# The head of the first feed-forward part in quarter pieces over two issuing queues, and the rounded half of a weight unit waited for alone

## What is computed

```
def swiglu(x, w_gate, w_up, w_down):
    return (jax.nn.silu(x @ w_gate) * (x @ w_up)) @ w_down
h = h + FFN_RES * swiglu(rms_norm(h, ffn1_norm[l]), ...)
h = h + hybrid_mixer(rms_norm(h, mix_norm[l]), ...)
h = h + FFN_RES * swiglu(rms_norm(h, ffn2_norm[l]), ...)
```

## Time and profile before

| | us |
|---|---|
| median of three runs | 1114.24 |
| profiled execution, its own time | 1114.35 |
| its span | 1112.5 |
| around the span | 1.85 |
| PE busy | 1106.8 (99%) |
| DVE busy | 790.6 (71%) |
| ACT busy | 621.2 (56%) |
| transfers, mean over the span | 187 GB/s |

### The profile page before, as it was taken

How to read it: one execution, slowest core, us unless ns; L and a number is a source line. 1 busy time by engine, 2 the same in 40 slices (tenths; PEclk the granted TensorE clock), 3 DMA queues, 4 the chain that set the end, 5 groups by cost and what they waited for, 6 DMA issues and landing times.

```text
span 1112.5 us, 14865 instructions
## 1 busy us (share of the span) xinstructions
PE 1106.8 (99%) x5830; PEld 941.2 (85%) x5830; DVE 790.6 (71%) x1136; ACT 621.2 (56%) x825; POOL 58.0 (5%) x105
## 2 busy tenths in 40 slices
PE   9999999999999999999999999999999999999998
PEld 8888888888888888888888888888877788888887
DVE  6777754667987677775477787557898786777752
ACT  6556542677656456554356556337787854656530
POOL 1000000100000000000000000011343000000000
PEclk9999999999999999999999999999999999999999
DMA  9755565654454665555565555557643455555541
GB/s 317 252 190 189 189 246 190 211 162 141 165 195 157 203 189 190 189 189 189 191 206 190 189 189 189 189 154 255 224 150 122 149 181 164 191 188 194 192 179 38
DMA packets 142581, 208.02 MB, mean 187 GB/s; under 512 B 9296, under 2 KB 100584, under 8 KB 142512
## 3 DMA queue, kind: packets, MB, share of 16 engines
q1 hardware_dynamic: 139408, 198.07, 52.7%
q0 software_dynamic: 3088, 9.00, 2.4%
q10 hardware_dynamic: 16, 0.00, 0.0%
HBM read 205.98 MB, written 2.65 MB: 188 GB/s over the span
## 4 chain that ended last, share of the span: by engine, by line
PE 98%; ACT 1%; DMA 0%; issue 0%; DVE 0%; SPq 0%; ACTq 0%; DVEq 0%
PE banks L1810 28%; PE banks L1696 16%; PE banks L1698 16%; PE banks L1697 16%; PE banks L1807 14%; PE banks L1768 1%; PE banks L2046 1%; PE banks L1718 1%; PE banks L1983 1%; DMA raw<-in_ffn_w_gate 0%; PE banks L2076 0%; PE banks L2073 0%; PE banks L2142 0%; PE banks L2016 0%; PE banks L2019 0%
## 5 line engine op out<-in xcount | busy, mean ns | idle before, releaser
L1143 DVE TENSOR_TENSOR w_lo<-raw,w_hi 128x2048 fp32r<-128x2048 f32 x186 | 422.7, 2275 | 167.8 <-ACT w_hi L752 167.5
L752 ACT ACTIVATE w_hi<-raw 128x2048 fp32r<-128x2048 f32 x186 | 352.2, 1897 | 111.8 <-PE banks L1698 108.2
L1810 PE MATMUL banks<-xT,w_hi 128*128 128x512 f32 x1344 | 314.5, 390 | 0.0
L1810 PEld LDWEIGHTS banks<-xT,w_hi 128*128 128x128 f32 x1344 | 249.2, 188 | 49.7
L1696 PE MATMUL banks<-w_hi,xT 128*128 128x512 f32 (+1 forms) x432 | 170.4, 394 | 0.0
L1807 PEld LDWEIGHTS banks<-xT,w_lo 128*128 128x128 f32 x1344 | 167.4, 191 | 3.4
L1807 PE MATMUL banks<-xT,w_lo 128*128 128x256 f32 x1344 | 169.8, 283 | 0.0
L1698 PE MATMUL banks<-w_hi,xT 128*128 128x512 f32 (+1 forms) x432 | 167.0, 387 | 0.0
L1697 PE MATMUL banks<-w_lo,xT 128*128 128x512 f32 (+1 forms) x432 | 166.7, 386 | 0.0
L1696 PE MATMUL banks<-w_hi,hT_hi 128*128 128x512 f32 x352 | 137.3, 390 | 0.0
L830 ACT ACTIVATE gate<-gate 128x256 f32<-128x256 f32 x84 | 35.1, 418 | 182.5 <-DVE gate L1272 182.5
(11 more groups left out here) (324 smaller groups left out, 900.1 us busy)
## 6 DMA issues: line engine op xcount, KB each, us to landing
raw<-in_ffn_w_gate SPq DMA_DIRECT2D x88, 512.0 KB, 3.7
raw<-in_ffn_w_up SPq DMA_DIRECT2D x88, 512.0 KB, 4.7
raw<-in_ffn_w_down SPq DMA_DIRECT2D x88, 512.0 KB, 4.1
raw<-in_w_in SPq DMA_DIRECT2D x76, 512.0 KB, 4.4
raw<-in_w_out SPq DMA_DIRECT2D x16, 512.0 KB, 4.0
raw<-in_w_branch_moba SPq DMA_DIRECT2D x4, 512.0 KB, 4.4
raw<-in_w_branch_sb SPq DMA_DIRECT2D x4, 512.0 KB, 4.9
raw<-in_w_branch_a SPq DMA_DIRECT2D x4, 512.0 KB, 4.2
```

The costliest lines, as they stand in the source:

```text
L752: act.activation(w_hi[u % SLOTS][:, 0:n], raw[u % RAWS][:, 0:n], ACT.Copy).then_inc(hi_done, 1)
L1143: dve.tensor_tensor(w_lo[r][:, 0:n], raw[r][:, 0:n], w_hi[u % SLOTS][:, 0:n], ALU.subtract).then_inc(lo_done, 1)
L1810: m = pe.matmul(bank[b + s], mh, xT[:, k].rearrange("p a s -> p (a s)"), start=first, stop=k == KC - 1, skip_group_check=c == 0)
```

## The change

1. x comes in four transfers of 256 columns instead of two of 512. The gate and up halves of unit 0 and 1 come in two pieces each (`load_first`, 256 KB), but unit 1's up pieces share one semaphore.
2. SP issues x's first quarter ahead of the identity. The gate half of unit 0 is issued by ACT, one piece ahead of the gain rows and one behind them.
3. PE transposes two column groups, starts on unit 0's gate after them, and takes the rest a quarter at a time. The second column group has a bank of its own (`first_bank`) and is rounded by DVE (`second_hi`).
4. ACT and DVE round and subtract the gate half of both units and the up half of unit 0 in pieces.
5. `pair_chunk` waits for `hi_done` of its first unit, and for `lo_done` only ahead of the products of `w_lo`, in 40 chunks.
6. GpSimd waits for `hi_done` of unit 3 ahead of the positions and tables too.

The core of the diff (semaphores, DVE's half and the removed functions left out):

```
...
+        def load_first(eng, u, s, i, signal):
+
+            w = a[ffn_w[0][s]].rearrange("(k p) (c n) -> p k c n", p=P, n=CH)
+            k = 4 * u + 2 * i
+            eng.dma_start((gate_half, up_half)[s](raw[u])[:, 2 * i:2 * i + 2, :], w[:, k:k + 2, 0, :]).then_inc(signal, 16)
+
+        def first_bank(k):
+
+            return bank[3][:, 0:SEQ] if k == 1 else bank[4 + k // 2][:, k % 2 * SEQ:(k % 2 + 1) * SEQ]
+
...
+            load_x(0)
             sp.dma_start(ident, a["consts"][:, 0:P]).then_inc(ident_in, 16)
-            load_x(0)
+            load_x(1)
+            for i in range(2):
+                load_first(sp, 0, 1, i, up_in[i])
+            for j in range(2, 4):
+                load_x(j)
+            for i in range(2):
+                load_first(sp, 1, 0, i, gate_in[1][i])
+            for i in range(2):
+                load_first(sp, 1, 1, i, raw_in[1])
...
             pool.memset(freq[:, 0:1], INV_FREQ[0]).then_inc(gained, 4)
+            pool.wait_ge(hi_done, 4)
...
+                    first_x_hi(0)
+                    act.wait_ge(first_half_hi[0], 1)
+                    gate_hi(0, 1)
+                    first_x_hi(1)
+                    for i in range(2):
+                        act.wait_ge(up_in[i], 16)
+                        act.activation(up_half(w_hi[0])[:, 2 * i:2 * i + 2, :], up_half(raw[0])[:, 2 * i:2 * i + 2, :],
+                                       ACT.Copy).then_inc(hi_done if i else up_hi, 1)
+                    for i in range(2):
+                        first_x_hi(2 + i)
+                        gate_hi(1, i)
+                    act.wait_ge(raw_in[1], landed(1))
+                    act.activation(up_half(w_hi[1]), up_half(raw[1]), ACT.Copy).then_inc(hi_done, 1)
...
             act.preload_act_table_set("silu_and_others")
+            load_first(act, 0, 0, 0, gate_in[0][0])
             act.dma_start(gain_rows, a[gains[0]].rearrange("(k p) -> k p", p=P)).then_inc(gain_row_in, 16)
+            load_first(act, 0, 0, 1, gate_in[0][1])
...
+                    dve.wait_ge(gate_in[0][0], 16)
+                    dve.tensor_copy(gate_half(w_hi[0])[:, 0:2, :], gate_half(raw[0])[:, 0:2, :]).then_inc(first_half_hi[0], 1)
+                    dve.wait_ge(second_turned, 1)
+                    dve.tensor_scalar(xT_hi[:, 1, :], first_bank(1), gain_cols[:, 1:2], None, ALU.mult).then_inc(second_hi, 1)
+                    for i in range(2):
+                        gate_lo(0, i)
+                        if i == 0:
+                            dve.wait_ge(second_hi, 1)
+                        first_x_lo(i)
...
+            def first_turn(j):
+
+                pe.wait_ge(x_in[j], 16)
+                for k in (2 * j, 2 * j + 1):
+                    for tt in range(TT):
+                        ins = pe.transpose(first_bank(k)[:, tt * P:(tt + 1) * P], x[:, tt, k * P:(k + 1) * P], ident)
+                    if k == 0:
+                        ins.then_inc(x_turned, 1)
+                    elif k == 1:
+                        ins.then_inc(second_turned, 1)
+                if j:
                     ins.then_inc(x_turned, 1)
+            def first_term(u, s, i, term):
+
+                j = 2 * u + i
+                if term == 0:
+                    pe.wait_ge(xT_hi_done, j + 1)
+                    if s == 0:
+                        pe.wait_ge(first_half_hi[u], i + 1)
+                    elif u == 0 and i == 0:
+                        pe.wait_ge(up_hi, 1)
+                    else:
+                        pe.wait_ge(hi_done, u + 1)
+                elif term == 1:
+                    if s == 0:
+                        pe.wait_ge(first_half_lo, j + 1)
+                    elif u == 0 and i == 0:
+                        pe.wait_ge(up_lo, 1)
+                    else:
+                        pe.wait_ge(lo_done, u + 1)
+                else:
+                    pe.wait_ge(xT_lo_done, j + 1)
+                last = u == 1 and s == 1 and term == 2 and i == 1
+                for k in (2 * j, 2 * j + 1):
+                    if k == 1 and s == 0 and term == 0:
+                        pe.wait_ge(second_hi, 1)
...
-                    first_columns(0, 0)
+                    first_term(0, 0, 0, 0)
                     first_turn(1)
-                    first_columns(0, 1)
-                    first_columns(1, 0)
-                    first_columns(1, 1)
+                    first_term(0, 0, 0, 1)
+                    first_term(0, 0, 0, 2)
+                    for term in range(3):
+                        first_term(0, 0, 1, term)
+                    first_term(0, 1, 0, 0)
+                    first_term(0, 1, 1, 0)
+                    first_turn(2)
+                    first_turn(3)
+                    first_term(0, 1, 0, 1)
+                    first_term(0, 1, 1, 1)
+                    first_term(0, 1, 0, 2)
+                    first_term(0, 1, 1, 2).then_inc(unit_used, 1)
+                    for s in range(2):
+                        for term in range(3):
+                            for i in range(2):
+                                m = first_term(1, s, i, term)
+                    m.then_inc(unit_used, 1)
...
                 u = BASE[ph] + 2 * c
-                pe.wait_ge(lo_done, u + 1)
+                pe.wait_ge(hi_done, u + 1)
                 for p in range(2):
                     pair_free(ph, c, p)
                     pair_products(ph, c, 0, p, False)
                 if c == 1 and ph not in FIRST_OF:
                     spread_rows(ph)
+                pe.wait_ge(lo_done, u + 1)
                 for p in range(2):
                     m = pair_products(ph, c, 0, p, True)
                 m.then_inc(unit_used, 1)
```

More of the change, by code:

```diff
@@ L327, in build @@
         tile_done = sem("tile_done")
-        first_half = [sem("first_half0"), sem("first_half1")]
+        gate_in = [[sem(f"gate_in{u}{i}") for i in range(2)] for u in range(2)]
+        up_in = [sem("up_in0"), sem("up_in1")]
+        up_hi = sem("up_hi")
+        second_turned = sem("second_turned")
+        second_hi = sem("second_hi")
+        up_lo = sem("up_lo")
         gain_row_in = sem("gain_row_in")
@@ L334, in build @@
         warm_set = sem("warm_set")
-        x_in = [sem("x_in0"), sem("x_in1")]
+        x_in = [sem(f"x_in{j}") for j in range(4)]
         ident_in = sem("ident_in")
@@ L579, in load_gate_up @@
                     w = a[ffn_w[f][s]].rearrange("(k p) (c n) -> p k c n", p=P, n=CH)
-                    put(u, slot[:, :, s * CH:(s + 1) * CH], w[:, 4 * hf:4 * hf + 4, c, :],
-                        first_half[u] if u < 2 and s == 0 else None)
+                    put(u, slot[:, :, s * CH:(s + 1) * CH], w[:, 4 * hf:4 * hf + 4, c, :])
             def load_rows(w, u, r0, rows, c0, width):
@@ L605, in _ @@
                     f = FFN_OF[ph]
-                    for c in range(1):
-                        for hf in range(2):
-                            load_gate_up(f, c, hf, u0 + 2 * c + hf)
-                            if ph == "F0" and hf == 0:
-                                load_x(1)
-                    for c in range(1, NCH):
+                    for c in range(ph == "F0", NCH):
                         for hf in range(2):
@@ L647, in zero_rest @@
                 ins.then_inc(zeroed, 1)
-            for n in range(2):
-                pool.wait_ge(x_in[n], 16)
+            for j in range(4):
+                pool.wait_ge(x_in[j], 16)
             pool.memset(freq[:, 0:1], INV_FREQ[0]).then_inc(gained, 4)
+            pool.wait_ge(hi_done, 4)
             for t in range(TT):
@@ L765, in first_x_hi @@
                 act.wait_ge(x_turned, j + 1)
-                for i in range(2):
-                    k = 2 * j + i
-                    ins = act.activation(xT_hi[:, k, :], bank[4 + j][:, i * SEQ:(i + 1) * SEQ], ACT.Copy,
-                                         scale=gain_cols[:, k:k + 1])
+                for k in (0,) if j == 0 else (2 * j, 2 * j + 1):
+                    ins = act.activation(xT_hi[:, k, :], first_bank(k), ACT.Copy, scale=gain_cols[:, k:k + 1])
                 ins.then_inc(xT_hi_done, 1)
@@ L840, in ffn, with gate_hi @@
                     act.wait_ge(gain_copied, 1)
[L841 to L851 removed]
+                    def gate_hi(u, i):
+                        k = slice(2 * i, 2 * i + 2)
+                        act.wait_ge(gate_in[u][i], 16)
+                        act.activation(gate_half(w_hi[u])[:, k, :], gate_half(raw[u])[:, k, :], ACT.Copy)\
+                            .then_inc(first_half_hi[u], 1)
+                    first_x_hi(0)
[11 more added lines that the diff above has]
+                    act.activation(up_half(w_hi[1]), up_half(raw[1]), ACT.Copy).then_inc(hi_done, 1)
                 else:
@@ new lines, in seam @@
+                    for i in range(2):
+                        k = slice(2 * i, 2 * i + 2)
+                        dve.wait_ge(hi_done if i else up_hi, 1)
```

(30 more changed lines are left out.)

74 lines of the change are left out of this document (15 added, 59 removed).

## The result

| | before | changed |
|---|---|---|
| median of 20 runs each, us | 1114.24 | 1115.90 |
| lowest to highest, us | 1114.00 to 1114.50 | 1115.24 to 1116.61 |
| profiled execution, us | 1114.35 | 1116.24 |
| its span, us | 1112.5 | 1114.4 |

The ratio is 1.0016 (95% interval 1.0010 to 1.0022): the changed kernel is 1.66 us slower. That is within the 0.2% to which the prediction gave 0.90, but 1.8 us above its 1114.1 and 0.5 above the top of its range, 1115.4. The spread has grown too, from 0.5 us to 1.4.

What follows compares the result with a forecast made beforehand. PE, busy 99% of the span, was taken as the bound. First product 0.9 us earlier, less 0.4 for four transposes and 0.4 for waits, left 0.1 us: median 1114.1 us, range 1113.4 to 1115.4.

Steps and rivals of the forecast that it cites:

- the 0.2% to which the prediction gave 0.90: Whole kernel: a measurement can't tell 0.2%, 2.2 us, from no change; chance 0.90 that the result lies within it.
- First transfers: Kernel start: gain rows and identity gate PE, both taken at 4.1 us, bounds 3.5 and 5.1.
- Warm-up: Behind the gain: three zero products, 1.3 us, formerly free while x was on its way, now stand on the path.
- late clock: Kernel start: PE idles some 1 us, so the clock may rise later; at 9.5, 1.0 us more, 1115.1; chance 0.14.
- two queues: First transfers: both queues share bytes, first product at 7.3, 1114.3 to 1114.7; at its end 7.7, 1114.9; chance 0.17.
- The head's row: First product to chunk 1: 12.8 us of products and transposes plus 0.95 of waits in place of 0.56.
- The moved wait at zero: Chunks of pairs: worth nothing by itself, as unit 2's remainder is ready at 19.8 and PE doesn't wait in other chunks.
- The second chain: Chain making the hidden values: unit 2 lands at 15.7, hidden values come 0.5 us earlier, at 25.5 and 25.9.
- Two even limits: First 27 us: PE's row and the hidden values' chain nearly even; PE earlier by itself would only wait at 26.
- GpSimd at zero: Positions and tables, 49 KB used at the end of F0, issued some 10 us later: zero effect.
- early data: Kernel start: gain at 3.5, unit 2 at 15.4; 0.4 to 0.8 us gained, 1113.3 to 1113.8; chance 0.17.
- what would show it: Timeline signs: gain's transpose near 4.1, first product near 6.85, chunk 1 near 20.6; wrong if first weight loads exceed 300 ns.

Runs made afterwards that it cites:

- the identity first: Changed kernel with the identity issued ahead of x's first quarter on SP, nothing else; 1115.14 us.
- both first: Changed kernel with the identity issued ahead of x's first quarter on SP and the gain rows ahead of the first gate piece on ACT; 1114.32 us.
- the early transposes: Changed kernel with the third and fourth pair of column groups transposed ahead of the first products of unit 0's up half; 1115.42 us.
- the gap filled: Changed kernel with nine zero products instead of five ahead of the gain's transpose; 1115.02 us.
- the kernel with both edits: Changed kernel with identity and gain rows issued first, and third and fourth pair of column groups transposed ahead of unit 0's up half; 1114.21 us.
- the reordering: Kernel with both edits, plus in F0 x's squares ahead of unit 2's rounding on ACT and the root ahead of unit 2's remainder on DVE; 1113.43 us.
- the gap in the kernel before: Kernel before without the three zero products between the gain's transpose and those of x; 1115.31 us.
- the kernel with one zero product fewer: The kernel with the reordering, with two zero products behind the gain's transpose instead of three; 1113.72 us.
- the moved wait alone: Kernel before with only the wait of the chunks of pairs moved; 1114.30 us.
- one queue: The kernel with both first, with unit 0's two gate pieces issued by SP, each behind a quarter of x; 1114.65 us.
- the two with the reordering in the kernel before: Kernel before with the same reordering of ACT and DVE in F0: with the moved wait 1114.21 us, without it 1116.23 us.

## Why the prediction was wrong, point by point

Against the working of the prediction, chunk 1 was reached at 22.60 instead of 20.6. The 2.0 us are 1.07 at the first product (7.92 for 6.85) and 0.93 in the row (14.68 for 13.75). Of these, 0.84 are the identity, 0.23 the way from it to the first product, 0.79 the clock behind that, and 0.14 are left. Either of the two large terms alone would have left the time inside the range (1115.2 with the whole 1.07, 1114.9 with the clock's 0.79); together they left it. (The profiled execution lies 0.34 above the median, so the median's 1.8 is made up a little differently.)

1. **First transfers: the step that failed.** Gain and identity were put at 4.1, between 3.5 and 5.1. The identity came at 4.95, close to the upper bound, and this is 0.84 of the 1.07 (gain's transpose at 4.99 for 4.15). The bound's argument was near the truth: x's first quarter landed at 4.1 (0.74 + 3.4), the first gate piece at 4.5 (0.76 + 3.7), and the small one that gates PE behind both. The value was taken nearer the other end because the gain had come in 2.7 us; but that was on an empty queue. The kernel with the identity first shows the identity's share, 0.76 us by the medians, that with both first the whole, 1.58.
2. **Warm-up and clock: a rival treated as an alternative.** The late clock was foreseen with its sign and price (a rise at 9.5 for 1.0 us more; it rose at about 9.6, and the row paid 0.79 behind the first product). In the sum itself the clock stood at nothing. It had a chance of 0.14 as a case by itself, beside "two queues". The runs show that they belong together: a late identity opens the gap (1.43 us), filling it gave the clock back by 5.3, and a gap of 1.52 in the kernel before cost 1.05 us. Two queues at its end, 1114.9, plus the 1.0 of the late clock, is 1115.9, the median measured; that it meets it to the tenth is luck, since the 1.0 measured 0.79 and the case at its end had the first product at 7.7. The forecast should have priced the clock at each arrival time of the identity, and the range should have reached to the sum.
3. **The head's row: right.** Without the clock's 0.79 its waits are 1.11 us, 0.33 in unit 0 and 0.78 at unit 1, where 0.95 were put. (The terms worked out, 0.2 and 0.7, make only 0.9.) The timeline names DVE's remainder for 0.18 of it, and the early transposes take 0.75 of the 0.78 away. The price of four more transposes, 0.42, was never measured by itself: the four behind the first products start 0.70 ahead of the next product at the low clock (8.92 to 9.62) and 0.35 ahead of it with the gap filled (7.71 to 8.06).
4. **The moved wait at zero: right**, for all 40 chunks together.
5. **The second chain: landing right, end off.** Unit 2 landed at 15.4 (6.94 + 8.5) where 15.7 was put. But ACT reached it only at 17.36, since the column groups of unit 1 were late with PE; so the chain was 1.15 later than before and not 0.5 earlier. It cost nothing, because PE was later still.
6. **Two even limits: right.** The claim that an earlier PE would only wait is what the kernel with both edits shows (0.63 us), and the reordering shows it from the other side: either limit alone brings 0.1 us or less, both bring 0.9.
7. **GpSimd at zero**: nothing in the waits of PE speaks against it; it was not tried alone.
8. **Room early on: misread.** For "early data" the prediction took 135 GB/s up to 5.1 us as a sign of room. That rate counts identity and x alone. All transfers together moved 59 GB/s in the first 3 us of the kernel before and 308 in the next 2 (75 and 341 in the changed kernel), with a mean busy share of 0.88 from 3 to 5 us before, so there was little room left from 3 us on.

Of what would show it, the loads of over 300 ns at the first products were named as the sign of an error, and that sign was there.

What stays open is what each execution's clock depends on. A gap of 1.4 to 1.5 us goes with a rise behind 9 us in all three traces that have one (the changed kernel, the early transposes, the gap in the kernel before). But gaps of 0.92 and 0.21 (the identity first, the gap filled) still left a spread of 1.3 and 1.1, and the kernel with one zero product fewer, with no such gap, one of 1.5. In eight traces (the kernel before, the moved wait alone, both small transfers first, both edits, one queue, the norm ahead of unit 2, and the two with the reordering in the kernel before) PE did the same work up to the transposes of x, with three zero products behind the gain and no gap over about 0.3: the rise lies between about 4.7 and 7.2 us in seven and at about 9.7 in one. No run here separates the length of a gap from its place and from the work ahead of it.

## What to carry to other kernels

Ahead of the first product, issue what gates everything first, however small it is: a 64 KB and a 4 KB transfer behind a bulk one cost 1.6 us here, while the second issuing queue was worth 0.33. An idle stretch of PE in its warm-up can be a cost of its own (about 1 us here for 1.5 us of idling), which has to be added to whatever makes the stretch longer, not weighed against it. Where two chains end within tenths of a microsecond of each other, undo or improve them together, since an experiment on either alone reads as "no effect".

## What the runs showed of the hardware

- The identity, 64 KB, landed 3.7 us after its issue behind a 256 KB transfer of its queue and beside another queue's, 2.3 with x behind it and a gate piece beside it, 2.0 with that piece behind the gain.
- The clock's granted share was 1.000 for the span of every trace, and for the first stretches too (1.00 from 3 to 9.6 us in the changed kernel), also where the clock rose at 9.6 us only. Only durations by line and time show which level the first products had.
- Leaving out three zero products, 1.3 us of work off the critical path, cost 1.05 us; adding four over the changed kernel's gap gave 0.88 back. Work that computes nothing can be on the path by what it does to the clock.
- The same work of PE up to 5 us was followed by a rise of the clock anywhere from about 4.7 us (both small transfers first) to about 9.7 (the kernel before with the reordering), and the latter cost 0.66 us up to chunk 1.
